# WKV preparation of a hybrid encoder block: four feature blocks as a pipeline, part of the k and r products on GpSimd

## What is computed

```
kk = (k * p['k_k']).reshape(B, T, H, N)
kk = kk / jnp.maximum(jnp.linalg.norm(kk, axis=-1, keepdims=True), 1e-12)
for d in range(2):
    w = jnp.exp(-DECAY_SCALE * jax.nn.sigmoid(p['decay_w0'][d] + jnp.tanh(xw @ p['decay_w1'][d]) @ p['decay_w2'][d]))
    a = jax.nn.sigmoid(p['aaa_a0'][d] + (xa @ p['aaa_a1'][d]) @ p['aaa_a2'][d])
    kd = k * (1.0 + (a - 1.0) * p['k_a'])
    y_sum = y_sum + wkv7_scan(rh, w.reshape(B, T, H, N), kdh, vh, -kk, kk * ah, reverse=(d == 1))
    bonus = bonus + jnp.sum(rh * kdh * p['r_k'], axis=-1, keepdims=True) * vh
```

## Time and profile before

| what | value |
|---|---|
| median of 3 runs | 2770.46 us (2763.62 to 2773.02) |
| the profiled execution | 2771.89 us, its span 2770.1 us |
| busy in the span | PE 2271.1, DVE 1157.1, ACT 763.7, POOL 334.7 us |
| granted TensorE clock, mean | 0.892 |

### The profile page before, as it was taken

How to read it: one execution, slowest core, us unless ns; L and a number is a source line. 1 busy time by engine, 2 the same in 40 slices (tenths; PEclk the granted TensorE clock), 3 DMA queues, 4 the chain that set the end, 5 groups by cost and what they waited for, 6 DMA issues and landing times. The chain is left out here.

```text
span 2770.1 us, 42284 instructions
## 1 busy us (share of the span) xinstructions
PE 2271.1 (82%) x17252; PEld 1898.2 (69%) x17252; DVE 1157.1 (42%) x1619; ACT 763.7 (28%) x1236; POOL 334.7 (12%) x352
## 2 busy tenths in 40 slices
PE   3899997944414768887579986969999999999999
PEld 2788882322203545555568865869999889999987
DVE  4343006646742356767357743422333223332221
ACT  3111110024413214444334422213222212222211
POOL 0000000000000019950544310000000000000000
PEclk9999999966756679999589956989999999999999
DMA  2222210024367210010377424432222333222222
GB/s 85 75 86 86 86 71 35 0 88 193 151 228 222 80 61 1 1 46 11 99 171 186 115 76 148 141 125 76 76 76 80 109 115 111 71 75 76 76 98 89
DMA packets 140716, 262.87 MB, mean 95 GB/s; under 512 B 11024, under 2 KB 89360, under 8 KB 138992
## 3 DMA queue, kind: packets, MB, share of 16 engines
q1 hardware_dynamic: 140592, 261.12, 28.8%
HBM read 189.18 MB, written 68.93 MB: 93 GB/s over the span
## 5 line engine op out<-in xcount | busy, mean ns | idle before, releaser
L203 PE MATMUL ff_acc<-normed_nh,ff_low 128*128 128x320 f32 x1408 | 436.1, 310 | 18.9 <-DVE ff_low L2318 17.7
L204 PE MATMUL ff_acc<-normed_nl,ff_high 128*128 128x320 f32 x1408 | 435.8, 310 | 0.0
L205 PE MATMUL ff_acc<-normed_nh,ff_high 128*128 128x320 f32 x1408 | 435.7, 309 | 0.0
L2318 DVE TENSOR_TENSOR ff_low<-ff_raw,ff_high 128x1024 fp32r<-128x1024 f32 x132 | 161.7, 1225 | 451.6 <-ACT ff_high L2280 451.4
L203 PEld LDWEIGHTS ff_acc<-normed_nh,ff_low 128*128 128x128 f32 x1408 | 264.9, 188 | 19.7 <-issue 19.7
L204 PEld LDWEIGHTS ff_acc<-normed_nl,ff_high 128*128 128x128 f32 x1408 | 265.0, 188 | 0.0
L205 PEld LDWEIGHTS ff_acc<-normed_nh,ff_high 128*128 128x128 f32 x1408 | 264.9, 188 | 0.0
L2280 ACT CAST ff_high<-ff_raw 128x1024 fp32r<-128x1024 f32 x132 | 138.0, 1046 | 255.4 <-PE ff_acc L205 234.0
L204 PE MATMUL ff_acc<-ff_low,ff_hh 128*128 128x512 f32 x440 | 171.2, 389 | 0.0
L203 PE MATMUL ff_acc<-ff_high,ff_hl 128*128 128x512 f32 x440 | 171.2, 389 | 0.0
L205 PE MATMUL ff_acc<-ff_high,ff_hh 128*128 128x512 f32 x440 | 171.2, 389 | 0.0
(11 more groups left out here) (250 smaller groups left out, 4296.8 us busy)
## 6 DMA issues: line engine op xcount, KB each, us to landing
dram_sx<-pr_sx SPq DMA_DIRECT2D x8, 2816.0 KB, 8.1
ff_raw<-in_w_gate SPq DMA_DIRECT2D x44, 512.0 KB, 3.2
ff_raw<-in_w_up SPq DMA_DIRECT2D x44, 512.0 KB, 3.2
ff_raw<-in_w_down SPq DMA_DIRECT2D x44, 512.0 KB, 3.5
si_ab<-dram_sx SPq DMA_DIRECT2D x44, 384.0 KB, 6.9
pj_packed<-in_w_in SPq DMA_DIRECT2D x24, 512.0 KB, 4.3
ch_ops<-dram_sx SPq DMA_DIRECT2D x88, 128.0 KB, 3.5
ch_ops<-dram_sx SPq DMA_DIRECT2D x44, 256.0 KB, 4.5
```

The source lines that it names most:

```text
L203: nc.tensor.matmul(out, ll, rh, start=start, stop=False)
L204: nc.tensor.matmul(out, lh, rl, start=False, stop=False)
L205: return nc.tensor.matmul(out, lh, rh, start=False, stop=stop)
L2318: nc.vector.tensor_tensor(low[s][:, :], raw[s][:, :], high[s][:, :].bitcast(F32), ALU.subtract).then_inc(cut_low[s], 1)
```

## The change

`prep` alone is rewritten; all else is the same text. What it does:

- **DVE.** The running sums of both directions (`sums_of`) come first in a block, then the bonus of the block before, then the two `kd` and the two a times kk, then the products into `sx`. `kk` of block f+1 (`norm_k`) is made between the products b and k of direction 1 of block f. The inverse is taken inside direction 0. The sum of the two `kd` and its product with r leave DVE; `1 + (a-1) k_a` leaves it for ACT.
- **POOL.** Has these two operations (L611, L614 of the kernel after), both 128x1408 with both inputs in SBUF. `r_k` is folded into `heads` ahead of time (`heads_rk`, four 128x128 operations on DVE at the start).
- **ACT.** `scale_a` makes `k_a*a + (1 - k_a)` as one activation for each direction. The buffer `e1` is gone: `exp` of the sum goes over `sg`. The root, the rows and the sigmoids of block f+1 stand at the end of block f.
- **PE.** The same products in another order: all of block f+1 before the bonus product of block f.
- **SP.** k, r and `w2` are loaded apart from v, those of block 0 ahead of the constants; block f+2's are loaded behind the store of `sx[1]` of block f; the bonus of a block is stored during the next one.

```diff
-                sp.dma_start(heads[:, :], g.small_of("heads")).then_inc(consts, 16)
+                def load_kr(f):
+                    s = f % 2
+                    if f >= 2:
+                        sp.wait_ge(ready, 2 * (f - 1))
+                        sp.wait_ge(kd_summed, f - 1)
+                    sp.dma_start(w2[s][:, :, :], g.lora2[f]).then_inc(kr_in[s], 16)
+                    for n, t in ((1, k), (0, r)):
+                        for a, ln, p in SEQS:
+                            row = (n * FT + f) * P
+                            sp.dma_start(t[s][:, p:p + ln], g.proj[row:row + P, a:a + ln]).then_inc(kr_in[s], 16)
...
+                def store_bonus(f):
+                    sp.wait_ge(bonus, f + 1)
+                    sp.dma_start(g.bonus[f * P:(f + 1) * P, :], kds[:, :]).then_inc(bonus_stored, 16)
+                sp.wait_ge(zeroed, 6)
+                load_kr(0)
...
                 for f in range(FT):
-                    if f + 1 < FT:
-                        load(f + 1)
-                    for d in range(2):
...
-                        sp.dma_start(g.sx[d, f], sx[d][:, :, :, :].rearrange("p c x t -> p (c x t)")).then_inc(stored, 16)
-                    sp.wait_ge(bonus, PRIMED + f + 1)
-                    sp.dma_start(g.bonus[f * P:(f + 1) * P, :], kds[:, :]).then_inc(stored, 16)
-                sp.wait_ge(stored, PRIMED + 48 * FT)
+                    if f >= 1:
+                        store_bonus(f - 1)
+                        if f + 1 < FT:
+                            load_v(f + 1)
+                    for d in both:
+                        sp.wait_ge(ready, 2 * f + d + 1)
+                        sp.dma_start(g.sx[d, f], sx[d][:, :, :, :].rearrange("p c x t -> p (c x t)")).then_inc(sx_stored[d], 16)
+                    if f + 2 < FT:
+                        load_kr(f + 2)
+                store_bonus(FT - 1)
...
+                for f in range(FT):
+                    s = f % 2
+                    pool.wait_ge(kd_ready, f + 1)
+                    if f:
+                        pool.wait_ge(bonus_stored, 16 * f)
+                    nc.gpsimd.tensor_tensor(kds[:, :], kd[0][:, :], kd[1][:, :], ALU.add).then_inc(kd_added, 1)
+                    pool.wait_ge(kd_added, f + 1)
+                    pool.wait_ge(kr_in[s], KR * (f // 2 + 1))
+                    nc.gpsimd.tensor_tensor(kds[:, :], r[s][:, :], kds[:, :], ALU.mult).then_inc(kd_summed, 1)
...
+                def for_w(f, d):
+                    pe.wait_ge(kr_in[f % 2], KR * (f // 2 + 1))
+                    if d or f == 1:
+                        pe.wait_ge(sig_w, 2 * f + d)
+                    elif f >= 2:
+                        pe.wait_ge(bonus, f - 1)
+                    product(psb, w2[f % 2][:, 2 * d, :], g.hid[:, 2 * d, :], w_prod)
...
+                def for_a(f, d):
+                    if d:
+                        pe.wait_ge(sig_a, 2 * f + 1)
+                    elif f:
+                        pe.wait_ge(normed, f + 1)
+                    product(psa, w2[f % 2][:, 2 * d + 1, :], g.hid[:, 2 * d + 1, :], a_prod)
...
+                def bonus_of(f):
+                    pe.wait_ge(kd_summed, f + 1)
+                    if f + 1 < FT:
+                        pe.wait_ge(sig_w, 2 * f + 4)
+                    else:
+                        pe.wait_ge(bonus, f)
+                    product(psb, heads_rk[:, f, :], kds, bonus_prod)
...
+                for_w(0, 0)
+                for_a(0, 0)
...
                 square_sums(0)
+                for_w(0, 1)
+                for_a(0, 1)
...
                 for f in range(FT):
...
+                        for_w(f + 1, 0)
                         spread_norms(f + 1)
+                        for_a(f + 1, 0)
+                        for_w(f + 1, 1)
+                        for_a(f + 1, 1)
+                    bonus_of(f)
...
+                def scale_a(f, d):
+                    act.wait_ge(sig_a, 2 * f + d + 1)
+                    if f:
+                        act.wait_ge(kd_added, f)
+                    nc.scalar.activation(kd[d][:, :], av[d][:, :], ACT.Identity, scale=par("k_a", f),
+                                         bias=without_a[:, f:f + 1]).then_inc(affine, 1)
...
+                    more = f + 1 < FT
+                    exponentials(f, 0)
+                    if more:
                         square(f + 1)
-                    for d in range(2):
-                        act.wait_ge(summed, PRIMED + 2 * f + d + 1)
...
+                    if more:
                         root(f + 1)
                         to_rows(f + 1)
+                        sigmoid_w(f + 1, 0)
+                        sigmoid_a(f + 1, 0)
+                        sigmoid_w(f + 1, 1)
+                        sigmoid_a(f + 1, 1)
+                        for d in both:
+                            scale_a(f + 1, d)
...
+                def norm_k(f):
+                    dve.wait_ge(kr_in[f % 2], KR * (f // 2 + 1))
+                    dve.wait_ge(spreads, f + 1)
+                    if f:
+                        dve.wait_ge(av_ready, 2 * f)
+                        dve.wait_ge(a_made, 2 * f)
+                    nc.vector.scalar_tensor_tensor(out=kk[:, :], in0=k[f % 2][:, :], scalar=par("k_k", f),
+                                                   in1=psa[:, 0:PTOK], op0=ALU.mult, op1=ALU.mult).then_inc(normed, 1)
+                    dve.wait_ge(normed, f + 1)
...
+                def sums_of(f, d):
+                    c3 = chunked(cs[d])
+                    dve.wait_ge(sig_w, 2 * f + d + 1)
+                    nc.vector.tensor_tensor_scan(cs[d][:, :], first[:, :], sg[d][:, :], 0.0, ALU.mult, ALU.add).then_inc(scanned, 1)
+                    dve.wait_ge(scanned, 2 * f + d + 1)
+                    nc.vector.tensor_copy(tot[:, d, :].unsqueeze(2), c3[:, :, CH - 1:CH])
...
-                    dve.wait_ge(stored, PRIMED + 48 * f)
-                    chained(nc.vector.tensor_tensor(kds[:, :], kd[0][:, :], kd[1][:, :], ALU.add))
-                    nc.vector.scalar_tensor_tensor(out=kds[:, :], in0=r[s][:, :], scalar=par("r_k", f), in1=kds[:, :],
-                                                   op0=ALU.mult, op1=ALU.mult).then_inc(scaled_r, 1)
...
+                for f in range(FT):
+                    s, more = f % 2, f + 1 < FT
+                    o = lambda d, x: sx[d][:, :, SLOT[d][x], :]
+                    sums_of(f, 0)
+                    if f == 0:
+                        floor(0)
+                    sums_of(f, 1)
+                    if f == 0:
+                        invert(0)
+                        norm_k(0)
+                    else:
+                        bonus_of(f - 1)
+                    for d in both:
+                        dve.wait_ge(affine, 2 * f + d + 1)
+                        last = tt(kd[d][:, :], kd[d][:, :], k[s][:, :], ALU.mult)
+                    last.then_inc(kd_ready, 1)
+                    for d in both:
+                        tt(av[d][:, :], kk[:, :], av[d][:, :], ALU.mult).then_inc(av_ready, 1)
+                    if more:
+                        floor(f + 1)
+                    for d in both:
...
+                        nc.vector.scalar_tensor_tensor(out=o(d, "a"), in0=chunked(kk), scalar=-1.0, in1=chunked(ex[d]),
+                                                       op0=ALU.mult, op1=ALU.mult).then_inc(a_made, 1)
+                        if d == 0 and more:
+                            invert(f + 1)
+                        dve.wait_ge(av_ready, 2 * f + d + 1)
+                        tt(o(d, "b"), chunked(av[d]), chunked(cs[d]), ALU.mult)
+                        if d == 1 and more:
+                            norm_k(f + 1)
+                        dve.wait_ge(kd_ready, f + 1)
+                        tt(o(d, "k"), chunked(kd[d]), chunked(cs[d]), ALU.mult)
+                        tt(o(d, "r"), chunked(r[s]), chunked(sg[d]), ALU.mult).then_inc(ready, 1)
+                bonus_of(FT - 1)
```

More of the change, by code:

```diff
@@ L539, in prep @@
         psa, psb, psq = c.ps("psa", (P, 3 * 512)), c.ps("psb", (P, 3 * 512)), c.ps("psq")
-        consts, zeroed = c.sem("consts"), c.sem("zeroed")
-        loaded = [c.sem(f"loaded{s}") for s in range(2)]
+        consts, zeroed, fixed = c.sem("consts"), c.sem("zeroed"), c.sem("fixed")
+        kr_in, v_in = ([c.sem(f"{n}{s}") for s in range(2)] for n in ("kr_in", "v_in"))
         squared, sums, floored, rooted, inverted, rows, spreads, normed = (
             c.sem(n) for n in ("squared", "sums", "floored", "rooted", "inverted", "rows", "spreads", "normed"))
[L545 to L549, removed]
+        w_prod, a_prod, sig_w, sig_a, affine = (c.sem(n) for n in ("w_prod", "a_prod", "sig_w", "sig_a", "affine"))
+        scanned, mirrored, summed, exped, scaled_up, ready = (
+            c.sem(n) for n in ("scanned", "mirrored", "summed", "exped", "scaled_up", "ready"))
+        kd_ready, av_ready, kd_added, kd_summed, bonus_prod, bonus = (
```

(23 more changed lines are left out.)

173 lines of the change are left out of this document (75 added, 98 removed).

## The result

The changed kernel took 2745.56 us in the median of 4 runs (2742.63 to 2751.38), the kernel before 2771.19 beside it: ratio 0.9915, 95% interval 0.9898 to 0.9933. So it is 0.85% faster, where I had forecast 1.8%: the gain is 25.6 us instead of 49.5. The profiled execution has a span of 2740.8 us.

What follows compares the result with a forecast made beforehand. Waits, no engine being full, bound prep. A block takes 33.3 us of DVE work plus 5.5 for POOL, 38.8; the last bonus ends at 743.5 instead of 793.0, gaining 49.5: 2771.9 - 49.5, less 1.4, is 2721 us; range 2702 to 2740.

Steps and rivals of the forecast that it cites:

- What bounds, and DVE's own work: In prep no engine is full, so waits set the length; DVE's own work falls from 38.3 to 33.3 us a block.
- POOL's turns: POOL and DVE alternate at SBUF beside a times kk and first `sx` products: 5.5 us a block, 22 over four.
- I take the first at half clock and 1 us of wait for each of three blocks: Next block's sigmoids: PE's first small product, a(0), at half clock, later ones at full clock; 3 us of waits in all.
- the 3 allowed: The 3 us of waits for PE in the forecast sum, 1 us for each of three blocks.
- The first block's chain: Block 0: first scan at 575.2, second group ends at 590, then inverse, rows, spread and kk exposed, to 598.4.
- PE stays at half clock: Rival, 12%: longer PE waits in three blocks and some 3 us more in the first block's chain: 2721 + 12 = 2733.
- The pipeline does not close: Rival, 3%: one engine's order, likely ACT's, hands lateness on; 13.9 us of gaps return in three blocks: 2721 + 42 = 2763.

Runs made afterwards that it cites:

- padding: The changed kernel with 64 more rows, all zero, in `hid` and `w2`, so prep's small products run over 128 rows: 2723.73 us, ratio 0.9852.

## Why the direction was right and the size wrong

- **What bounds, and DVE's own work: right.** The rest of block 0, from kk on, took 26.4 us, forecast 26.1; of periods of 43.9 and 44.1 the waits are 5.4, which leaves 38.5 and 38.7 against 38.8. The last bonus ends at 767.76 instead of 793.0, 25.2 us earlier, and the medians differ by 25.6: the barriers pass the gain on whole.
- **POOL's turns: right.** Lost by the pairs 4 x 3.0, by the product at L816 2.86, 1.97, 2.19 and 2.95 (3.03, 2.14, 2.36 and 3.12 less 0.17), 21.9 us in all, forecast 22. Without POOL's reads both go back to 3.15 and 0.17. The Trainium skill, SBUF — State Buffer, section Who interferes with whom, says that a VectorE instruction with two SBUF inputs contends with a GpSimd instruction that reads SBUF, for ports that they lock against each other. The trace agrees, and here the wait lasts to the end of POOL's operation, down to 128x22 elements that wait 2.9 us.
- **The step that failed: "I take the first at half clock and 1 us of wait for each of three blocks".** That a(0) would be at half clock was right (forecast 4.5, measured 5.06 us). But the sum took w(1) and a(1) behind it, and in the first block all behind w(0), at full clock, from the earlier trace rows, where they run directly behind a 128-row spread in which the clock has risen. The change takes that away: the first block's products now come first, out of 13.8 us of idling, and a(0) waits 2.84 us for kk (3.81 and 3.71 in the later blocks). They took 4.9 to 5.1 us, and none got faster while PE was busy; with 128 rows those behind the first did. Price: per block 3.36 + 1.3 to 1.6 and 0.6 to 0.8 at L753, 5.4 us in blocks 1 and 2 and 5.0 in block 3, instead of 1. Against the forecast lengths, which hold no wait, that is 10.5 us over blocks 1 and 2 and 5.6 over block 3, less the 3 allowed; and in the first block from the first scan to the end of the second group 6.2 us more than forecast (21.0 instead of 14.8).
- **The first block's chain: a second, smaller omission.** Its first scan came 2.5 us late (loads at 571.1, not 569.3, and a product of 5.06, not 4.5). Behind the second group two ACT scalings (3.00 us) and a table load (1.28 us) stand ahead of the root, and DVE waits 2.62 us for it; the sum had no wait there. The stretch from the group's end to the end of kk took 10.6 us instead of 8.4. The whole: 2.5 + 6.2 + 2.2 = 10.9.
- **Sum of the miss:** 10.9 + 0.3 + 10.5 + 5.6 - 3 = 24.3 us, of which padding returns 17 to 22. With padding the kernel takes 2723.7 against the forecast 2721, and in its profile the last bonus ends at 748.0 instead of 743.5: the rest of the sum stands to within 5 us. That the time comes closer than the stage is luck: the profiled execution was 3.4 us shorter outside the stage than that of the kernel before.
- **The rival "PE stays at half clock" was the right one,** at 12%, and under-priced at 12 us: it counted the products' lateness, but neither the norm sums at L753 nor the first block's five pieces in a row, where each piece at half clock is 2.4 us late and DVE has nothing else to do.
- **"The pipeline does not close" is out:** k and r are in time, and blocks 1 to 3 show no wait ahead of L765.

The Trainium skill, TensorE: Matmul & The Clock Gate, Part 1, ties the clock to how busy the engine has lately been and counts no rows. If busy is read as time without a gap, this case's trace does not agree for products of 64 rows: 24 us, and no rise.

**What stays open.** Why 64-row products at full clock stay there in some blocks and fall back in others behind gaps of 0.57 and 0.97 us; how long PE had been at full clock before the gap differs between these blocks and was not varied alone. Only 64 and 128 rows were tried, nothing between. And the 24 us of the first block contain the norm sums, of 128 rows but two columns each, which did not raise the clock either; they were not tried alone.

## What to carry to other kernels

Take a matmul's duration only from a row whose neighbours are those it will have after the change: if a change moves short products away from the full-height work in front of them, price all of them at half clock first, and count what waits for each. If products have less than 128 rows and come after a wait, zero rows up to 128 can be worth trying: 17 to 22 us here, and nothing where the products already followed full-height work. An elementwise operation given to POOL is not off DVE's path when DVE reads two SBUF inputs beside it: here it cost DVE 2.7 us on average (21.9 us over eight operations), and 1.6 us done by DVE itself.

## What the runs showed that I had not expected

Of TensorE: 64-row products ran at 1.2 GHz for 24 us without idle time, and the same with 64 zero rows were at 2.4 GHz behind the first of 4.41 us; 128-row products kept 2.4 GHz over gaps of 2.16 and 2.52 us, where a 64-row one fell back behind 2.27 us. Of the turns: an operation of 22 columns on DVE takes 3.03 us beside POOL instead of 0.17, and one of 1408 columns loses as much (3.0): in these rows what is left of POOL's operation sets the loss, not the size of DVE's. And of the 22 us that the turns take from DVE, leaving out POOL's reads returned 17 by the medians, with and without padding: other waits take up the rest, above all for the norm sums (some 3.6 us in a middle block without padding, 2.8 with it).
